# Early weight tiles of three joins: preparation moved ahead of the evictions, bias sums regrouped, a third PSUM bank

## The reference

```
for l in range(2):
    h = rms_norm(x) * norm1_w * (1 + sc1) + sh1          # shift and scale from a condition vector
    x = x + g1 * (mixer(h @ w_in) @ w_out)               # w_in: 1024 x 4096, 32 column tiles
    h = rms_norm(x) * norm2_w * (1 + sc2) + sh2
    a = h @ w_gate; v = h @ w_val                        # 1024 x 2816 each
    x = x + g2 * ((silu(conv3(a)) * v) @ w_down)
return rms_norm(x) * final_norm_w
```

## Time and profile before

| what | value |
|---|---|
| median of 3 runs | 2204.47 us (2202.11 to 2207.41) |
| the profiled execution, its own time | 2207.13 us |
| its span | 2205.8 us |
| PE busy | 2084.3 us, 94% |
| joins A, B, C, from the first early matmul to the start of tile 6 | 44.55, 52.55, 43.73 us |

### The profile page before, as it was taken

The page is one execution under the profiler, slowest core; times in us unless marked ns, Lnnn a source line. Parts: engine busy times, 40 slices in busy tenths (PEclk is TensorE's granted clock), DMA queues, the critical chain, the costliest instruction groups (busy, mean ns, idle before and its releaser), DMA issues.

```text
span 2205.8 us, 26490 instructions
## 1 busy us (share of the span) xinstructions
PE 2084.3 (94%) x10486; PEld 1740.3 (79%) x10486; DVE 1370.3 (62%) x1873; ACT 882.3 (40%) x1365; POOL 194.2 (9%) x197
## 2 busy tenths in 40 slices
PE   4999989989999989999999999998999998999998
PEld 2788878877787777888887888886888887888886
DVE  7666767575666766775476635656685467643554
ACT  3356665224667524223353313335322355322321
POOL 0201011211101222000000000000000000000000
PEclk9999999989999999999999999998999999999999
DMA  8312221224212255443225434532534233433332
GB/s 292 110 58 68 60 65 58 79 75 139 77 59 85 87 164 164 122 129 86 76 78 171 138 109 137 153 112 89 166 102 134 59 95 115 134 111 96 99 95 78
DMA packets 312811, 238.31 MB, mean 108 GB/s; under 512 B 7024, under 2 KB 290032, under 8 KB 312048
## 3 DMA queue, kind: packets, MB, share of 16 engines
q1 hardware_dynamic: 293536, 166.87, 25.7%
q0 software_dynamic: 18432, 67.12, 9.9%
q10 hardware_dynamic: 720, 2.62, 0.3%
HBM read 234.49 MB, written 2.10 MB: 107 GB/s over the span
## 4 chain that ended last, share of the span: by engine, by line
PE 81%; DVE 7%; ACT 5%; issue 3%; DMA 2%; SPq 1%; POOL 0%; DVEq 0%; ACTq 0%; POOLq 0%
PE ps L624 62%; PE ps L597 4%; PE ps L2348 2%; PE ps L1358 1%; ACT a_p L1624 1%; PE ps L1339 1%; PE ps L1340 1%; DMA mod_w_out<-in_ada_w_turned 1%; PE ps L1369 1%; PE ps L2329 1%; DMA start_mod_rows<-in_w_mod_turned 1%; PE ps L2426 1%; ACT L1624 1%; PE ps L1229 1%; PE ps L2415 1%
## 5 line engine op out<-in xcount | busy, mean ns | idle before, releaser
L624 PE MATMUL ps<-h_second_hi,w_hi_second 128*128 128x512 f32 x1120 | 452.4, 404 | 17.9 <-ACT w_hi_second L560 17.9
L624 PE MATMUL ps<-h_second_lo,w_hi_second 128*128 128x512 f32 x1120 | 441.4, 394 | 0.0
L624 PE MATMUL ps<-h_second_hi,w_lo_second 128*128 128x512 f32 x1120 | 277.1, 389 | 0.0
L580 DVE TENSOR_TENSOR w_lo_second<-w_raw_second,w_hi_second 128x1024 fp32r<-128x1024 f32 x160 | 196.8, 1230 | 114.8 <-ACT w_hi_second L560 114.7
L624 PEld LDWEIGHTS ps<-h_second_hi,w_hi_second 128*128 128x128 f32 x1120 | 213.7, 191 | 64.5 <-ACT w_hi_second L560 19.2
L624 PEld LDWEIGHTS ps<-h_second_lo,w_hi_second 128*128 128x128 f32 x1120 | 213.7, 191 | 44.7 <-issue 1.9
L624 PEld LDWEIGHTS ps<-h_second_hi,w_lo_second 128*128 128x128 f32 x1120 | 210.3, 188 | 44.5
L624 PE MATMUL ps<-h_hi,w_hi_first 128*128 128x512 f32 (+1 forms) x592 | 209.3, 367 | 3.0 <-ACT proj L1489 1.7
L624 PE MATMUL ps<-h_lo,w_hi_first 128*128 128x512 f32 (+1 forms) x592 | 202.9, 356 | 0.0
L560 ACT ACTIVATE w_hi_second<-w_raw_second 128x1024 fp32r<-128x1024 f32 x168 | 176.0, 1049 | 34.1 <-PE ps L624 25.0
L2733 ACT ACTIVATE conv<-ps,cols 128x512 f32<-128x512 f32 x44 | 34.4, 781 | 269.5 <-PE ps L624 268.8
(11 more groups left out here) (326 smaller groups left out, 3811.3 us busy)
## 6 DMA issues: line engine op xcount, KB each, us to landing
w_raw_second<-in_w_in SPq DMA_DIRECT2D x64, 512.0 KB, 4.5
w_raw_first<-in_w_in SPq DMA_DIRECT2D x48, 512.0 KB, 3.9
mod_w_mixer<-in_ada_w_turned POOLq DMA_DIRECT2D x47, 512.0 KB, 4.1
w_raw_second<-in_w_gate SPq DMA_DIRECT2D x44, 512.0 KB, 3.9
w_raw_second<-in_w_val SPq DMA_DIRECT2D x44, 512.0 KB, 4.7
w_raw_down<-in_w_down SPq DMA_DIRECT2D x32, 704.0 KB, 4.9
mod_w_ffn<-in_ada_w_turned POOLq DMA_DIRECT2D x32, 512.0 KB, 4.1
mod_w_in<-in_w_mod_turned POOLq DMA_DIRECT2D x27, 512.0 KB, 4.0
```

Of the source, the lines that this page charges most:

```text
L580: k.nc.vector.tensor_tensor(lo, raw, hi.bitcast(F32), ALU.subtract).then_inc(k.sem.weight_split_v, 1)
L624: last = tensor.matmul(k.ps[:, bank, 0:count], w[:, q * P:(q + 1) * P], rows[q][:, first:first + count], start=(n == 1), stop=(n == 3 * t.k))
```

## The change

At all three joins: tiles 4 and 5 are rounded on ACT inside the norm (tile 4 ahead of the last row of h, tile 5 after the bias is copied) and split on DVE between the three scalings of the early products; the loops that evict start to round and split at tile 6. Tile 5 (the value tile of pair 2 in `ffn`) goes to PSUM bank 7 in place of bank 1. The sum of the bias products is three additions of halves in place of one reduction, with a wait behind each of the first two; at joins A and C the third sum stands behind the split of tile 2 in place of ahead of the last eviction of the stage before.

At join B alone: the lags are (0, 6, 8) in place of (0, 3, 5), the sums of squares stand at step 5 and the spread at step 6; the bias products of tiles 1 and 2 are made inside the norm, and their sums in turns 4 and 8 of DVE's row loop; SP holds the loads of tiles 4 and 5 until these products are made; the condition's SiLU stands at tile 4, and two modulation chunks move from tiles 3 and 4 to tiles 11 and 15.

```diff
-                add(("in2", l), n, KT, 1, self.weight_tile("w_in_2", l, n), h2, only_x(EARLY_BANKS[i] if l and i < 3 else 7 if i == 2 else i % 2), "a")
+                add(("in2", l), n, KT, 1, self.weight_tile("w_in_2", l, n), h2, only_x(EARLY_BANKS[i] if l and i < 3 else 7 if i == (5 if l else 2) else i % 2), "a")
...
-                        add(("ffn", l, half), i, KT, 1, self.weight_tile(name, l, half * FFH + i), h2, only_x(EARLY_BANKS[2 * i + j] if half == 0 and 2 * i + j < 3 else j), "v")
+                        add(("ffn", l, half), i, KT, 1, self.weight_tile(name, l, half * FFH + i), h2, only_x(EARLY_BANKS[2 * i + j] if half == 0 and 2 * i + j < 3 else 7 if half == 0 and (i, j) == (2, 1) else j), "v")
...
-            for i in sorted([*range(3, 24), *((13, 17) if l == 0 else (9, 13, 17))]):
+            for i in sorted([*range(3, 24), 13, 17] if l == 0 else [*range(5, 24), 9, 11, 13, 15, 17]):
...
 def linear_sync(k, stage, first=0):
-    for u in k.stage_tiles[stage][first:]:
+    for i, u in enumerate(k.stage_tiles[stage][first:]):
+        if stage == early_stage(4) and i in (4, 5):
+            k.nc.sync.wait_ge(k.sem.bias_product, early(4)[1] + i - 2)
         load_tile(k, u)
...
-EARLY_LAGS = (0, 3, 5)
-
-EARLY_SUMS, EARLY_SPREAD = 3, 4
+EARLY_LAGS = {3: (0, 3, 5), 4: (0, 6, 8), 5: (0, 3, 5)}
+
+EARLY_SUMS, EARLY_SPREAD = {3: 3, 4: 5, 5: 3}, {3: 4, 4: 6, 5: 4}
...
 def bias_vector(k, call, n):
     s, vector = k.sem, k.nc.vector
     vector.wait_ge(s.bias_product, early(call)[1] + n + 1)
-    vector.tensor_reduce(k.bias_sums[:, n, :], k.bias_products[n % 2][:, :].rearrange("p (q m) -> p m q", q=KT), AX,
-                         ALU.add).then_inc(s.bias_reduced, 1)
+    products = k.bias_products[n % 2]
+    for size in (512, 256):
+        settle_vector(k, vector.tensor_tensor(products[:, 0:size], products[:, 0:size], products[:, size:2 * size], ALU.add))
+    vector.tensor_tensor(k.bias_sums[:, n, :], products[:, 0:P], products[:, P:2 * P], ALU.add).then_inc(s.bias_reduced, 1)
...
     norm_root(k, call, TX)
+    if call == 4:
+        bias_scalar(k, call, 1)
     for q in range(KT):
-        if q == 5:
-            round_tile(k, own[3])
+        if q == 3 and call == 4:
+            bias_scalar(k, call, 2)
+        if q in (5, 7):
+            round_tile(k, own[3 + (q == 7)])
...
     scalar.activation(k.early_bias, k.ps[:, 2, 4:7], ACT.Copy).then_inc(s.bias_ready, 1)
+    round_tile(k, own[5])
...
     split_tile_vector(k, own[2])
+    if call != 4:
+        bias_vector(k, call, 2)
     norm_invert(k, call, TX)
...
+        if call == 4 and turn in (4, 8):
+            bias_vector(k, call, turn // 4)
     split_tile_vector(k, own[3])
     vector.wait_ge(s.early_moved, biases // 3 + 1)
     for n in range(3):
+        if n:
+            split_tile_vector(k, own[3 + n])
...
-            if i in BIAS_ROWS:
+            if i in BIAS_ROWS and (call != 4 or i == BIAS_ROWS[0]):
                 bias_scalar(k, call, BIAS_ROWS.index(i))
...
-            if i > BIAS_ROWS[0]:
+            if i == BIAS_ROWS[1] or i > BIAS_ROWS[1] and call != 4:
                 bias_vector(k, call, BIAS_ROWS.index(i) - 1)
-            if i == BIAS_ROWS[2]:
-                bias_vector(k, call, 2)
...
-        if i >= len(SECOND_LAGS):
+        if i >= (5 if l else len(SECOND_LAGS)):
             round_tile(k, u + 1)
...
-        if i == 2:
+        if i == (4 if l else 2):
             silu_conditions(k, 2, 3 + 2 * l, (0,))
...
-        if i + 1 < len(own) and (l == 0 or i >= 3):
+        if i + 1 < len(own) and (l == 0 or i >= 5):
             split_tile_vector(k, own[i + 1])
...
-            linear_vector(k, ("ffn", l, half), ffn_vector(k, l, half), first=0 if half else 3)
+            linear_vector(k, ("ffn", l, half), ffn_vector(k, l, half), first=0 if half else 5)
```

More of the change, by code:

```diff
@@ L683, in ready @@
         tensor.wait_ge(s.early_low, rows + q + 1)
-    for step in range(KT + EARLY_LAGS[-1]):
-        for n, lag in enumerate(EARLY_LAGS):
+    lags = EARLY_LAGS[call]
+    for step in range(KT + lags[-1]):
+        for n, lag in enumerate(lags):
             if 0 <= step - lag < KT:
                 multiply_rows(k, own[n], 0, (step - lag,), ready, None, s.early_spent if n == 2 else None)
-        if step == EARLY_SUMS:
+        if step == EARLY_SUMS[call]:
             tensor.wait_ge(s.early_summed, rows + KT)
@@ L692, in early_tensor @@
             last.then_inc(s.norm_summed, 1)
-        if step == EARLY_SPREAD:
+        if step == EARLY_SPREAD[call]:
             tensor.wait_ge(s.norm_inverted, call + 1)
@@ L2883, in scalar_program @@
         for half in (0, 1):
-            linear_scalar(k, ("ffn", l, half), True, ffn_scalar(k, l, half), None if half else (3, 4 + 2 * l), 0 if half else 3)
+            linear_scalar(k, ("ffn", l, half), True, ffn_scalar(k, l, half), None if half else (3, 4 + 2 * l), 0 if half else 5)
             if half and l == 0:
```

## The result

| what | before | after |
|---|---|---|
| median beside each other | 2205.24 us (2202.11 to 2207.41) | 2192.57 us (2190.50 to 2194.03) |
| ratio, 95% interval | | 0.9943 (0.9926 to 0.9960) |
| the profiled execution, its own time | 2207.13 us | 2191.93 us |
| its span | 2205.8 us | 2190.6 us |
| joins A, B, C, first early matmul to tile 6 | 44.55, 52.55, 43.73 us | 38.57, 41.29, 40.81 us |

The change makes the kernel 12.6 us faster (0.57%; the interval gives 8.8 to 16.3). Forecast were 22.9 us and a range of 2176 to 2190. The sign was right, the size was not, and 2192.57 lies above the range.

A forecast was written before the change was run, and what follows sets the result against it. PE, busy 94% of the span, was taken as the bound, so only its waits and clock could give time back. Savings of 12.3 us at A and C and 10.6 at B made 2204.5 - 22.9 = 2182 us, range 2176 to 2190.

The forecast's parts named there:

- All waits for `w_hi_second` at tile 4: All three joins: PE's waits for ACT's rounding, 17.9 us in 3 waits, would be gone.
- The bias wait at B: Join B: PE waits 4.2 us for DVE's third bias sum, plus 2.8 us of low clock; tile 6 at 42.0.
- The tree: Bias sums on DVE: three additions take 1.4 us against 1.99 for a reduction, saving 0.5 us a sum.
- Bank 7: Tile 5 at A and C: in bank 1 it would wait until 34.4 for a product instead of starting at 29.8.
- The lags: Early matmuls of join B: with lag 6, tile 1's split is wanted at 4.9, so the 3.56 us wait goes.
- The step that failed: ACT at A and C: the condition vector's SiLU follows its DMA issue by 4.3 us, so it ends at 32.0 to 33.0.
- The chain: A and C: scalings, splits, taps and SiLUs ahead of bank 0 put tile 6 at 37.0, a wait of 1.8 us.
- the clock behind tile 6: A and C: low clock after the new 1.8 us wait costs 0 to 2.8 us, taken as 1.0 at each.
- rival 3: Evictions at the joins come late, costing 3 us per us of delay; 2210 us at 10 us; chance 0.03.
- Rival 2: Shorter evictions: waits at tile 6 and the bias sums vanish or halve; 2177 us or a little less; chance 0.15.
- The fourth rival: A and C: half the wait moves from tile 4 to tile 6, chain 3 us longer; 2190 us; chance 0.12.
- The first rival: All joins: every new wait, the 1.8 us ones too, puts PE at 1.2 GHz for a tile; 2185 to 2186; chance 0.2.

The follow-up runs named there:

- experiment 10: The changed kernel itself, unaltered, measured and profiled once more: 2191.72 us, 0.9928 of the kernel before.
- experiment 4: The changed kernel with tile 5 of each first FFN half back in PSUM bank 1: 2198.16 us, 0.9960 of the kernel before.
- experiment 5: The changed kernel with join B's lags and its steps of sums and spread put back as before: 2191.60 us, 0.9932.
- experiment 1: The changed kernel with the condition vector's DMA in the two FFNs issued at the start of the norm: 2185.76 us, 0.9904.
- experiment 2: The changed kernel with SP holding tile 7's load in each first FFN half until the condition vector has landed: 2185.37 us, 0.9902.
- experiment 7: The changed kernel with the condition's DMA issued early in the FFNs and join B's bias matmuls behind tile 3: 2180.23 us, 0.9875.
- experiment 9: The kernel of experiment 7 measured again, beside experiment 8 and experiment 10: 2183.32 us, 0.9889 of the kernel before.
- experiment 8: The kernel of experiment 7 with ACT's SiLU of the condition moved ahead of the eviction of tile 1: 2177.14 us, 0.9858.
- experiment 3: The changed kernel with each tree of three additions put back to one reduction: 2192.57 us, 0.9942 of the kernel before.
- experiment 6: The changed kernel with join B's bias matmuls behind tile 3 and the third bias sum behind that tile's split: 2189.91 us, 0.9921.

## Why the prediction went wrong

**What held.** All waits for `w_hi_second` at tile 4 went, as said, and the split's at B. The bias wait at B was forecast at 4.2 us and measured 4.19, released by DVE's sum. Its exactness is part luck, since both its ends came 0.35 us later than counted. The clock fell with it as forecast, and tile 6 came at 41.29 (42.16 in experiment 10) where 42.0 stood. The tree was taken at 1.4 us and took 1.39 (the 1.2 that followed from the Trainium skill, VectorE: DVE Perf Modes, "The DRAIN you can't avoid", is not what the rows show: the first two additions alone take 1.18 us to the start of the third, for 0.69 and 0.42); the spread's wait at 0.3 us and was 0.16. Bank 7 was said to replace a start of tile 5 behind pair 1's product, and experiment 4 shows it. The loads held at B and the chunks moved to tiles 11 and 15 cost nothing that shows: no wait in the list of PE's waits after belongs to them. The lags were credited with ending the 3.56 us wait; experiment 5 shows that it ends without them.

**The step that failed** is "its DMA is issued with the table load, and its SiLU began 4.3 us later, so 27.6 + 4.4 = 32.0 to 33.0". The chain was right in its order, down to the condition vector being on it. But the 4.3 us is the duration of a transfer next to the traffic of the kernel before, and the change itself moved the traffic: the earlier splits release three raw buffers, and SP issues three loads of 512 KB in the 5.6 us ahead of the vector's DMA. I counted the loads that the change holds at B, and not those that it releases at A and C. The duration became 5.27 and 7.49 us in this profile, 6.95 and 7.58 in experiment 10. Experiments 1 and 2 show the cause, from the vector's side and from the loads' side.

**The second term** is the clock behind tile 6: 1.0 us taken at each, a value between two rows. It was 1.67 after 2.81 us and 2.47 after 5.04. Even the wait of 1.84 us that I had forecast costs it in five of the six joins that have it (A and C of experiments 1, 7 and 9): tile 6 then takes 7.1 to 7.2 us for 5.44.

**The third** is the chain itself: 37.6 without the DMA (experiment 1), and 37.9 with one of 4.6 us (experiment 2), where I had 37.0.

Some sums of the prediction are loose, without changing its result. From 35.1, two taps of 0.75 end at 36.6, not 36.9. The undisturbed start of tile 6 is 16.3 + 16.3 + 2.4 = 35.0, written 35.1 and 35.2; PE's work turned out to be 35.6. In rival 3, the 24.9 / 3 is not the forecast gain of 22.9 by three. Rival 2's terms make 10.4 us, of which its 2177 is half. And the bounds named for 2179 to 2185, all taken to one side, reach further than that (2 x 1.8 us of clock and 1 us of chain at each join alone make 2189), but not to 2192.57.

The account to the start of tile 7, where the forecast is 43.4 at A and C (37.0 + 1.0 + 5.44) and 47.4 at B (42.0 + 5.44):

| term | A | B | C |
|---|---|---|---|
| chain 0.6 longer | 0.6 | | 0.6 |
| condition's DMA | 1.0 | | 3.2 |
| more low clock | 0.7 | | 1.5 |
| bias wait, tiles 3 to 5 | | -0.7 | |

That is 6.8 us in sum before rounding, of 10.3 between forecast and result. The DMA's entries are the starts of tile 6 less 37.6; the clock's are tile 6's length less 5.44 and less the 1.0 taken. Another 2.5 us are the two profiled executions' places among their runs: the one of before lay 1.9 us above its median, the one of after 0.6 below. The rest, under 1 us, I can't place. Counted with experiment 10's windows instead, the joins exceed the forecast by 4.8, 0.2 and 5.3 us, 10.3 in sum: the usual wait at A is near C's, from the same cause, and B was forecast right.

**Which case came true.** The fourth rival, "the wait moves from tile 4 to tile 6 by half at A and C (chain 3 us longer)", had 0.12 and 2190 us. Its size is right, its reason was not given: it spoke of a longer chain, and the 3 us are a DMA in it. The first rival (the clock falls after each wait) held as well, so that two cases that were priced apart came together; the upper end of the range took each alone. The text had named the sign to look for, tile 6 waiting 5 us, and it is what C shows. The signs named for tile 4 and for join B came as listed; the waits near 2 us at tile 6 did not, nor C's window of 37 to 39 us (40.81).

## What to carry to other kernels

When work is moved earlier, list not only what it frees on its engine but which buffers it releases, which DMAs that starts, and whose transfer is then in flight: a DMA's time read from the trace before holds only beside the traffic of before. A vector on the critical path is issued where nothing waits for it yet; here one issue moved gives some 7 us (experiment 1). And a wait of PE is priced with the slow stretch behind it, so that removing its last microsecond (experiment 8) gives more than that microsecond.

## What the runs showed of the hardware

**Transfers side by side.** The broadcast of the condition vector (512 KB) took 4.3 to 4.6 us from its issue to its use when the last weight load before it was issued 3.9 to 5.6 us ahead (the kernel before and experiment 2). It took 5.3 to 7.7 us with three issued in the 5.6 us ahead, in the twelve places of the six profiles that have this: the changed kernel's and those of experiments 3, 4, 5, 6 and 10. The windows from issue to use at C, after and (the second fence) before, columns as above:

```profile
1836.06:1843.55 7.49, 7.49 (x34) 5.89 (x32) 3.22 (x5) 3.17 (x4) 1.09 (x2) 1.00 0.82 273
```

```profile
1848.44:1852.76 4.32, 0.00 (x0) 0.00 (x0) 2.36 (x4) 4.02 (x5) 1.09 (x2) 0.72 0.65 229
```

The DMA engines were busy for 0.82 of the longer one at 273 GB/s, for 0.65 of the shorter one at 229; 2.0 MB were moved against 1.0 MB. The DMA queues in the same windows (packets, MB, share of the 16 engines' time), after and then before; q10 is the condition vector's, q1 the weight loads' and q0 that of POOL's loads of modulation data, of which two are issued 0.4 and 1.0 us behind the vector's in both kernels:

```profile
q0 software_dynamic: 277, 1.01, 34.0%
q1 hardware_dynamic: 1003, 0.50, 24.5%
q10 hardware_dynamic: 144, 0.52, 23.0%
```

```profile
q10 hardware_dynamic: 144, 0.52, 37.1%
q0 software_dynamic: 119, 0.47, 28.4%
```

Before, no packet of a weight load moved in the window. After, the last 0.50 MB of the three loads did, in packets of some 500 bytes. POOL's loads moved more as well. They stand at the same place in experiment 2, whose DMA took 4.63 us, so they alone don't make it long. What decides between 5.3 and 7.7 us with all loads issued at the same distances is not shown.

**The clock after a short wait.** In experiment 9 joins A and C are alike to 0.01 us up to tile 6, with a wait of 1.85 us in both, and the clock fell in one of them only. The first two rows are A, the others C:

```profile
1171.70 0.47 PE L624 MATMUL ps<-h_second_hi,w_hi_second 128*128 128x512 f32 x1 [1.85 <-DVE conv L2785]
...
1177.24 0.39 PE L624 MATMUL ps<-h_second_hi,w_hi_second 128*128 128x512 f32 x1
...
1837.47 0.47 PE L624 MATMUL ps<-h_second_hi,w_hi_second 128*128 128x512 f32 x1 [1.85 <-DVE conv L2785]
...
1838.93 0.58 PE L624 MATMUL ps<-h_second_hi,w_hi_second 128*128 128x512 f32 x1
1839.31 0.63 PE L624 MATMUL ps<-h_second_lo,w_hi_second 128*128 128x512 f32 x1
...
1844.66 0.39 PE L624 MATMUL ps<-h_second_hi,w_hi_second 128*128 128x512 f32 x1
```

Tile 6 took 5.54 us at A and 7.19 at C, with a granted clock of 1.00 and 0.76 over the tile. The fall comes 1.5 us after PE has started again, not in the wait. So both kinds of row in the prediction (2.30 us with no fall, 1.84 us with one) can be had from one wait, and its length alone does not tell which it will be; what else decides, these runs don't show. The Trainium skill (TensorE: Matmul & The Clock Gate, "What's actually happening") says that the activity is watched in windows that run free of the kernel's own timing. By that the same wait would fall differently into them at A and at C; no run here moved a wait to try it.
